# A 5th down-projection chunk as 7 block products, with the inner rows split into parts during the gate products

## The reference

```python
def swiglu_ffn(x, w_gate, w_up, w_down):
    return (jax.nn.silu(x @ w_gate) * (x @ w_up)) @ w_down      # D_FF = 2816

x = x + 0.5 * swiglu_ffn(rmsnorm(x, ffn1_norm), ...)            # ffn(0)
x = x + hybrid_mixer(rmsnorm(x, mix_norm), w_in, ...)           # attention and pooling
x = x + 0.5 * swiglu_ffn(rmsnorm(x, ffn2_norm), ...)            # ffn(1)
```

## Time and profile before

| | |
|---|---|
| Median of 3 runs | 703.39 us (703.12 to 704.21) |
| The profiled execution's own time | 703.74 us |
| Its span (first to last instruction) | 701.9 us |
| Granted TensorE clock, mean | 0.997 of full speed |
| TensorE busy | 692.2 us, 99% of the span |
| VectorE, ScalarE, GpSimd busy | 529.3, 397.4, 98.2 us |
| Read from HBM | 127.79 MB |

### The profile page before, as it was taken

How to read it: one execution, slowest core, us unless ns; L and a number is a source line. 1 busy time by engine, 2 the same in 40 slices (tenths; PEclk the granted TensorE clock), 3 DMA queues, 4 the chain that set the end, 5 groups by cost and what they waited for, 6 DMA issues and landing times.

```text
span 701.9 us, 9837 instructions
## 1 busy us (share of the span) xinstructions
PE 692.2 (99%) x3716; PEld 590.1 (84%) x3716; DVE 529.3 (75%) x774; ACT 397.4 (57%) x536; POOL 98.2 (14%) x72
## 2 busy tenths in 40 slices
PE   8999999999999999999999999999999999999995
PEld 7888888888888788888888888888888888888884
DVE  6797779989876556876679989976762747898756
ACT  6865545576377656644555566487444625576441
POOL 0022204000001300022205000000007072140002
PEclk9999999999999999999999999999999999999998
DMA  9987552348465334754552438564763273543001
GB/s 342 359 347 262 197 194 98 142 154 322 138 263 202 120 99 150 261 181 180 183 197 102 176 122 329 210 252 169 239 242 115 82 285 134 170 161 130 1 1 60
DMA packets 21109, 129.34 MB, mean 184 GB/s; under 512 B 2504, under 2 KB 3664, under 8 KB 6864
## 3 DMA queue, kind: packets, MB, share of 16 engines
q1 hardware_dynamic: 19728, 127.51, 49.7%
q10 hardware_dynamic: 1344, 1.34, 0.6%
HBM read 127.79 MB, written 1.06 MB: 184 GB/s over the span
## 4 chain that ended last, share of the span: by engine, by line
PE 97%; DVE 1%; DMA 1%; ACT 0%; SPq 0%; issue 0%; POOL 0%; POOLq 0%; DVEq 0%
PE ps L502 24%; PE ps L467 16%; PE ps L469 15%; PE ps L468 15%; PE ps L508 13%; PE ps L487 1%; PE ps L762 1%; DMA raw<-in_first 1%; PE ps L661 1%; PE ps L1114 1%; PE ps L933 1%; PE ps L521 1%; PE ps L491 1%; PE ps L817 1%; PE ps L818 1%; PE ps L819 1%
## 5 line engine op out<-in xcount | busy, mean ns | idle before, releaser
L1671 DVE TENSOR_TENSOR wlo<-raw,whi 128x2048 fp32r<-128x2048 f32 (+1 forms) x77 | 173.7, 2267 | 23.9 <-ACT whi L1191 23.7
L1191 ACT ACTIVATE whi<-raw 128x2048 fp32r<-128x2048 f32 (+1 forms) x86 | 161.3, 1879 | 40.5 <-PE ps L469 37.3
L502 PE MATMUL ps<-xt,whi 128*128 128x512 f32 x752 | 180.1, 391 | 0.0
L502 PEld LDWEIGHTS ps<-xt,whi 128*128 128x128 f32 x752 | 138.1, 188 | 26.7
L467 PE MATMUL ps<-whi,xt 128*128 128x512 f32 (+2 forms) x340 | 135.0, 397 | 0.1
L469 PE MATMUL ps<-whi,xt 128*128 128x512 f32 (+2 forms) x340 | 130.1, 383 | 0.0
L468 PE MATMUL ps<-wlo,xt 128*128 128x512 f32 (+2 forms) x340 | 129.9, 382 | 0.0
L508 PEld LDWEIGHTS ps<-xt,wlo 128*128 128x128 f32 x752 | 96.4, 191 | 3.7
L508 PE MATMUL ps<-xt,wlo 128*128 128x256 f32 x752 | 97.5, 283 | 0.0
L1594 POOL TENSOR_TENSOR wlo<-raw,whi 128x2048 fp32r<-128x2048 f32 (+1 forms) x9 | 41.0, 4558 | 290.1 <-ACT whi L1191 290.1
L1754 DVE TENSOR_TENSOR wlo<-raw,whi 128x2048 fp32r<-128x2048 f32 x32 | 75.7, 2366 | 1.2
(11 more groups left out here) (259 smaller groups left out, 776.8 us busy)
## 6 DMA issues: line engine op xcount, KB each, us to landing
raw<-in_gu SPq DMA_DIRECT2D x41, 1024.0 KB, 4.8
raw<-in_dn SPq DMA_DIRECT2D x22, 1024.0 KB, 4.7
raw<-in_win SPq DMA_DIRECT2D x8, 1024.0 KB, 4.8
raw<-in_fqk SPq DMA_DIRECT2D x8, 1024.0 KB, 4.8
raw<-in_wout SPq DMA_DIRECT2D x4, 1024.0 KB, 5.4
raw<-in_fg SPq DMA_DIRECT2D x4, 1024.0 KB, 7.3
raw<-in_fv SPq DMA_DIRECT2D x4, 1024.0 KB, 4.7
raw<-in_fo SPq DMA_DIRECT2D x4, 1024.0 KB, 4.8
```

The source lines that it names most:

```text
L502: return pe.matmul(ps[:, banks[u], :], wh[:, k * S + u * P:k * S + (u + 1) * P], x, start=k == 0, stop=k == KD - 1)
L1191: act.activation(whi[:, c % RING, w], raw[:, c % RING, w], ACT.Copy).then_inc(hi_ready, 1)
L1671: dve.tensor_tensor(wlo[:, c % RING, w], raw[:, c % RING, w], whi[:, c % RING, w].bitcast(F32), ALU.subtract).then_inc(lo_ready, 1)
```

## The change

`SEVEN` becomes (1, 3, 5, 7, 8), so g = 8 too takes two down slots; the down stage has 16 slots, with g = 8 in 12 and 13, g = 9 in 14 and g = 10 in 15. The high parts of steps 0 to 7 get eight places in the room of `par` (the mixers' parameters), the low parts overwrite the inner rows in `work`, and steps 8 to 10 use the three places of `hth`. So nothing waits for a buffer, and the parts of steps 0 to 7 are made inside the gate loop: step 2j - 1 in pass 4j, step 2j - 2 in pass 4j + 2. Since a low part overwrites rows that GpSimd reads, it waits for `s_sum` where the step is in `SEVEN`. The sums of inner rows for g = 8 are the fifth on GpSimd and stand ahead of its `weight_sums` for g = 1. `par` is loaded behind chunk 4 of the mixer's first weights, once `resid_done` says that the first FFN is over.

```diff
-SEVEN = (1, 3, 5, 7)
+SEVEN = (1, 3, 5, 7, 8)
...
+        h_hi = h_high[:, :].rearrange("p (g c) -> p g c", g=8)
+        h_lo = h_low[:, :].rearrange("p (g s) -> p g s", g=NG)
...
-            sp.dma_start(par[:, :], a["par1"]).then_inc(par_landed, 16)
...
                 chunk(C_WIN + i, a["win"][i])
+                if i == 4:
+                    sp.wait_ge(resid_done, 4)
+                    sp.dma_start(par[:, :], a["par1"]).then_inc(par_landed, 16)
...
-                    pe.wait_ge(ht_lo, ND * f + g + 1)
+                    pe.wait_ge(ht_lo, ND * f + max(g + 1, 8))
...
+                def looped_hi(j, back):
+
+                    act.wait_ge(h_done, NG * f + 4 * j - 2 * back + 2)
+                    act.activation(h_hi[:, bass.ds(2 * j - back, 1), :].rearrange("p g c -> p (g c)"),
+                                   h_sb[:, bass.ds(4 * j - 2 * back, 2), :].rearrange("p g s -> p (g s)"), ACT.Copy).then_inc(ht_hi, 1)
...
                         silu(j, i)
-                for g in range(HTS):
-                    hidden_hi(g)
+                        if i % 2 == 0:
+                            looped_hi(j, i // 2 + 1)
+                hidden_hi(8)
...
+                    if i == 0:
+                        hidden_hi(9)
...
                 input_sums_hi(0)
+                hidden_hi(10)
                 for g in range(ND - 1):
-                    if g + HTS < ND:
-                        hidden_hi(g + HTS)
...
+                def looped_lo(j, back):
+
+                    dve.wait_ge(ht_hi, ND * f + 2 * j + back - 2)
+                    if back == 1:
+                        dve.wait_ge(s_sum, 4 * NS * f + 4 * j)
...
-                for g in range(HTS):
-                    hidden_lo(g)
+                        if i % 2 == 0:
+                            looped_lo(j, i // 2 + 1)
+                hidden_lo(8)
...
+                    if i == 0:
+                        hidden_lo(9)
...
                 input_sums_lo(0)
-                weight_sums(dve, f, 1)
+                then_sums(RING - 1)
+                hidden_lo(10)
                 for g in range(ND - 2):
                     if g in SEVEN:
                         lo(C_DN[f] + place(g) + RING)
-                    if g + HTS < ND:
-                        hidden_lo(g + HTS)
+                        then_sums(place(g) + RING)
                     if g in SEVEN[:-1]:
                         input_sums_lo(SEVEN.index(g) + 1)
...
+                if SEVEN[-1] == ND - 3:
+                    products_out()
```

More of the change, by code:

```diff
@@ L168, in build @@
         hth = sb("hth", [P, HTS, BANK], F32R)
+        with nc.sbuf_tensor("more_sums", [P, HTS, BANK], F32) as more_sums:
+            pass
         htl = sb("htl", [P, HTS, BANK], F32R)
         gains = sb("gains", [P, 4, D])
+        with nc.sbuf_tensor("h_high", [P, PA_N], F32R) as h_high:
+            pass
         par = sb("par", [P, PA_N])
+        with nc.sbuf_tensor("h_low", [P, NG * S], F32R) as h_low:
+            pass
         work = sb("work", [P, 7700])
@@ L213, in build, with hidden_high @@
         s_sums = XN[:, :, :].rearrange("p t n -> p (t n)").rearrange("p (j n) -> p j n", j=4)
-        sums_hi = [xt[:, 2 * j:2 * j + 2, 0, :] for j in range(NS)]
-        sums_lo = [xt[:, 2 * j:2 * j + 2, 1, :] for j in range(NS)]
+        s_sums_of = [s_sums[:, j, :] for j in range(4)] + [more_sums[:, 2, :]]
+        sums_hi = [xt[:, 2 * j:2 * j + 2, 0, :] for j in range(4)] + [htl[:, 0, :].rearrange("p (k s) -> p k s", k=2)]
+        sums_lo = [xt[:, 2 * j:2 * j + 2, 1, :] for j in range(4)] + [htl[:, 1, :].rearrange("p (k s) -> p k s", k=2)]
+        h_hi = h_high[:, :].rearrange("p (g c) -> p g c", g=8)
+        h_lo = h_low[:, :].rearrange("p (g s) -> p g s", g=NG)
+        def hidden_high(g):
+            return h_hi[:, g, :] if g < 8 else hth[:, g - 8, :]
         part_sum = view(work, NG * S, BANK)
@@ L703, in given @@
                         col = (k * NT + t) * P
-                        return hth[:, g % HTS, col:col + P], htl[:, g % HTS, col:col + P]
+                        return hidden_high(g)[:, col:col + P], h_lo[:, 2 * g + k, t * P:(t + 1) * P]
                     def summed(i):
@@ L732, in down @@
                         m = three(ps[:, DOWN + 2 * nb + t, :],
-                                  hth[:, g % HTS, col:col + P], htl[:, g % HTS, col:col + P],
+                                  hidden_high(g)[:, col:col + P], h_lo[:, 2 * g + k, t * P:(t + 1) * P],
                                   wh[:, w], wl[:, w], g == 0 and k == 0, g == ND - 1 and k == 1)
@@ L1237, in hidden_hi @@
                 def hidden_hi(g):
-                    if g >= HTS:
-                        act.wait_ge(chunk_used, C_DN[f] + last_of(g - HTS) + 1)
                     act.wait_ge(h_done, NG * f + 2 * g + 2)
-                    act.activation(hth[:, g % HTS, :], h_sb[:, 2 * g:2 * g + 2, :].rearrange("p g s -> p (g s)"), ACT.Copy).then_inc(ht_hi, 1)
+                    act.activation(hidden_high(g), h_sb[:, 2 * g:2 * g + 2, :].rearrange("p g s -> p (g s)"), ACT.Copy).then_inc(ht_hi, 1)
+                def looped_hi(j, back):
+                    act.wait_ge(h_done, NG * f + 4 * j - 2 * back + 2)
+                    act.activation(h_hi[:, bass.ds(2 * j - back, 1), :].rearrange("p g c -> p (g c)"),
+                                   h_sb[:, bass.ds(4 * j - 2 * back, 2), :].rearrange("p g s -> p (g s)"), ACT.Copy).then_inc(ht_hi, 1)
                 if f == 0:
@@ L1282, in input_sums_hi @@
                         act.wait_ge(chunk_used, C_DN[f])
-                    act.activation(sums_hi[j], s_sums[:, j, :].rearrange("p (k s) -> p k s", k=2), ACT.Copy).then_inc(ss_hi, 1)
+                    act.activation(sums_hi[j], s_sums_of[j].rearrange("p (k s) -> p k s", k=2), ACT.Copy).then_inc(ss_hi, 1)
                 input_sums_hi(0)
+                hidden_hi(10)
                 for g in range(ND - 1):
-                    if g + HTS < ND:
-                        hidden_hi(g + HTS)
                     if g in SEVEN:
@@ L1599, in input_sums @@
                 (a11, a21), (a12, a22) = ([h_sb[:, 2 * g + k, t * P:(t + 1) * P] for t in range(NT)] for k in range(2))
-                s1, s2, s3, s4 = (s_sums[:, j, i * P:(i + 1) * P] for i in range(4))
+                s1, s2, s3, s4 = (s_sums_of[j][:, i * P:(i + 1) * P] for i in range(4))
                 before = 4 * (NS * f + j)
@@ L1726, in hidden_lo @@
                     dve.wait_ge(ht_hi, ND * f + g + 1)
-                    dve.tensor_tensor(htl[:, g % HTS, :], h_sb[:, 2 * g:2 * g + 2, :].rearrange("p g s -> p (g s)"), hth[:, g % HTS, :].bitcast(F32),
-                                      ALU.subtract).then_inc(ht_lo, 1)
+                    if g in SEVEN:
+                        dve.wait_ge(s_sum, 4 * (NS * f + SEVEN.index(g) + 1))
+                    dve.tensor_tensor(h_lo[:, 2 * g:2 * g + 2, :].rearrange("p g s -> p (g s)"), h_sb[:, 2 * g:2 * g + 2, :].rearrange("p g s -> p (g s)"),
+                                      hidden_high(g).bitcast(F32), ALU.subtract).then_inc(ht_lo, 1)
+                def looped_lo(j, back):
+                    dve.wait_ge(ht_hi, ND * f + 2 * j + back - 2)
+                    if back == 1:
+                        dve.wait_ge(s_sum, 4 * NS * f + 4 * j)
+                    pair = bass.ds(4 * j - 2 * back, 2)
+                    dve.tensor_tensor(h_lo[:, pair, :].rearrange("p g s -> p (g s)"), h_sb[:, pair, :].rearrange("p g s -> p (g s)"),
+                                      h_hi[:, bass.ds(2 * j - back, 1), :].rearrange("p g c -> p (g c)").bitcast(F32), ALU.subtract).then_inc(ht_lo, 1)
                 sum_halves(0, 0)
@@ L1765, in input_sums_lo @@
                     dve.wait_ge(ss_hi, NS * f + j + 1)
-                    dve.tensor_tensor(sums_lo[j], s_sums[:, j, :].rearrange("p (k s) -> p k s", k=2), sums_hi[j].bitcast(F32), ALU.subtract).then_inc(ss_lo, 1)
+                    dve.tensor_tensor(sums_lo[j], s_sums_of[j].rearrange("p (k s) -> p k s", k=2), sums_hi[j].bitcast(F32), ALU.subtract).then_inc(ss_lo, 1)
                 def half(t, nb, p, scale=0.5):
@@ L1795, in products_out, with then_sums @@
                     ordered(dve.scalar_tensor_tensor(out=second, in0=part_sum.unsqueeze(1).broadcast_to([P, 2, BANK]), scalar=0.5, in1=second, op0=ALU.mult, op1=ALU.add))
+                def then_sums(slot):
+                    for j in range(1, NS):
+                        if place(SEVEN[j]) == slot + 1:
+                            weight_sums(dve, f, j)
                 input_sums_lo(0)
-                weight_sums(dve, f, 1)
+                then_sums(RING - 1)
+                hidden_lo(10)
                 for g in range(ND - 2):
@@ L1808, in ffn @@
                         lo(C_DN[f] + last_of(g) + RING)
-                    if g in SEVEN[:-2]:
-                        weight_sums(dve, f, SEVEN.index(g) + 2)
+                        then_sums(last_of(g) + RING)
+                if SEVEN[-1] == ND - 3:
```

(1 more changed line is left out.)

## The result

The changed kernel takes 707.12 us (median of 5 runs, 706.90 to 707.51); before took 704.16 over its 5 runs, the 3 shown above and 2 made beside the changed kernel. The ratio is 1.0045, 95% interval 1.0030 to 1.0059: slower by 0.45%, where 706.5 us and 0.44% were forecast. In a later set the changed kernel stood at 1.0052 (1.0039 to 1.0066). The spans of the profiled executions, 705.5 and 701.9, differ by 3.6 us, where the sum gave 3.1. The granted clock is 0.998, before it was 0.997.

What follows compares the result with a forecast made beforehand. TensorE, busy 99% of the span, was taken to bound the kernel. Per FFN -0.74 + 1.0 + 1.3 = +1.56 us, +3.1 in all, giving 706.5 us against 703.39, slower by 0.44%, range 704.3 to 709.2.

Steps and rivals of the forecast that it cites:

- The gain: TensorE's down stage: three matmuls fewer, -0.68 us, and the 0.06 wait in seven(7) gone; -0.74 us per FFN.
- The first gap: seven(1): TensorE waits for the sums' low part, as GpSimd's later weight sums delay DVE in pass 19; 1.0 us per FFN.
- The second gap: seven(8): TensorE waits for the sums' low part, queued behind lo of slot 14 on DVE; 1.3 us per FFN.
- the gate loop: Parts made inside the gate loop: DVE and ACT have room for them in the passes; 0 us.
- the load of `par`: Mixers' parameters, 2 MB, loaded late: lands early enough to be hidden, with the DMA engines nearly idle; 0 us.
- The rest of the down stage: Down stage outside the two gaps: DVE's load hardly grows and products_out comes no later against TensorE; 0 us.
- Only the second gap: Rival: DVE has caught up by seven(1), so only seven(8) waits; +0.56 us per FFN, 704.5 us; chance 0.13.
- no gap: Rival: sums' low parts come in time in seven(1) and seven(8), only matmuls count; 701.9 us, faster; chance 0.09.
- `par` in the way: Rival: the parameters' load delays the mixer's chunks 5 to 7, TensorE short 2 to 4 us; 708.5 to 710.5; chance 0.06.
- Whole blocking: Rival: DVE loses all 5.38 us of GpSimd's additions, gap in seven(1) 2.3; +2.9 per FFN, 709.2 us; chance 0.10.

Runs made afterwards that it cites:

- e3_both: Changed kernel with both reorderings: sums' parts for g = 8 ahead of slot 14, GpSimd's weight sums ahead of its fifth input sums; 701.97 us, 0.9979 of before.
- e8_dve_sums_second: Changed kernel with sums' parts for g = 8 ahead of slot 14, and weight sums of g = 1 on DVE instead of GpSimd; 701.88 us, 0.9979 of before.
- e9_both_again: e3_both repeated on another chip: the changed kernel with both reorderings; 701.93 us, 0.9975 of before.
- e4_four: Changed kernel without its fifth step: g = 8 an ordinary step again, the rest of the change kept; 703.34 us, 0.9997 of before.
- e2_first: Changed kernel with only GpSimd's order changed: weight sums for g = 1 ahead of the fifth input sums; 704.87 us, 1.0018 of before.
- e7_dve_sums: Changed kernel with the weight sums of g = 1 moved from GpSimd to DVE, behind pass 19; 704.75 us, 1.0023 of before.
- e5_late_parts: Changed kernel with DVE's two added low parts, hidden_lo(8) and hidden_lo(9), moved behind input_sums_lo(0); 706.19 us, 1.0039 of before.
- e1_second: Changed kernel with only the order at g = 7 changed: sums' high and low parts for g = 8 ahead of slot 14's; 704.61 us, 1.0009 of before.
- e6_more_load: Changed kernel with three more 0.5 MB loads behind that of par, whose readers wait for them too; 707.24 us, 1.0055 of before.

## Why the prediction was right

**The gain.** -0.74 per FFN was forecast. No run shows it alone, but e3_both, e8_dve_sums_second and e9_both_again, which have no gap, lie 1.5 to 1.6 us below before, against twice 0.74. The 0.06 in it is gone as well (e4_four).

**The first gap.** Taken at 1.0, measured 1.26. The mechanism was as written: pass 19, beside L370, and e2_first and e7_dve_sums close it by moving or removing GpSimd's additions. The term that was mis-sized is DVE's loss in pass 19: 4.02 was carried over from pass 17, it was 8.25 - 3.86 = 4.39. `times_row` alone makes the difference, 2.86 instead of 2.50: it began 0.46 us behind GpSimd's first addition then (108.09 to 108.55) and only 0.09 behind it now (119.42 to 119.51), so it met more of it. GpSimd was that late because its fifth input sums had met DVE's low part of pass 18: L1625 took 0.91, where the same line takes 0.46 in pass 16, and DVE's L1759 took 0.95 instead of 0.69. The sum allowed 0.1 to 0.3 for that meeting as time of DVE; this time itself did no harm, as DVE stood 0.60 ahead of pass 19, and the delay of GpSimd did. The low part of the sums ended at 136.97, for 136.75 in the text, and TensorE's second matmul followed 0.40 later, for 0.39. The rest of the difference is TensorE itself, which in this trace was 0.16 us earlier than in that of before. What the section does not say is that the two low parts, 1.2 us in its sum, are as much a condition of the gap as GpSimd's place: without them it is 0.06 (e5_late_parts).

**The second gap.** Worked out as 1.3, measured 1.35, and e1_second closes it by the order of the queue alone. The step said that it doesn't hang on how late DVE is otherwise, save for a bound of 1.5 with DVE 0.2 late. That was too strong: in e5_late_parts DVE came later and the gap was 1.89.

**Costs put at nothing.** All held: the gate loop and the load of `par` (e4_four, e6_more_load). `par` landed in 7.2 to 7.7 us. For the gate loop, DVE did stand 2.14 us for GpSimd's sums at the end of pass 16, where 1.6 was taken, and no one waited for it. The rest of the down stage was put at nothing as well and held in the changed kernel, but e5_late_parts shows how near to its end that room is.

**The rivals.** Only the second gap, and no gap, are refuted by the trace, and both exist as kernels: e2_first (1.0018) and e3_both (0.9979). `par` in the way is refuted by e6_more_load. Whole blocking was to show as 5.38 lost and a first gap of 2.3; it was 4.39 and 1.26. That refutes the price and not the rule: the additions' recorded durations sum to 5.39, but L372 began 0.47 us before `times_row` had ended and L374 0.20 before `hidden` had, so GpSimd's durations seem to hold waits of its own and can't be added up as DVE's loss. By the Trainium skill (SBUF — State Buffer, Who interferes with whom) the loser blocks for the whole instruction. The trace agrees: `times_row` began 0.09 behind L370 and ended 0.55 behind its end, `lo` began 0.13 behind L374 and ended 2.15 behind its end. Each is 0.14 short of what the instruction takes alone (0.69 and 2.29).

**The size.** The sum gave 3.1, the balance of the trace is 3.7, the spans 3.6, the medians 3.0 to 3.8. That the first ratio, 1.0045, meets the forecast of 0.44% to a hundredth is luck: the two gaps were taken 0.31 us per FFN too small, before stood at 704.16 in this comparison and not at the 703.39 that the forecast started from, and the changed kernel stood at 1.0052 in the next set. The 0.2% by which the kernel could have been faster was lost to two new waits, each as long as almost two such gains.

## What to carry to other kernels

When a step is made cheaper on the bounding engine, look in each helper's queue at what stands ahead of the one instruction that the shortened step waits for; moving it ahead of one copy and one subtraction was worth 2.8 us here, twice the gain of the whole change. Putting two shortened steps next to each other takes away the long step that had stood between them; that this long step had hidden the helper's chain is read from the order of the queue, and no run here has the fifth step in another place. And work given to GpSimd isn't free for DVE: count what DVE loses beside it before counting what it saves.

## What the runs showed of the hardware that was not expected

Three additions (one of 1024 and two of 512 elements per partition, float32, from and to SBUF) take DVE 2.58 us. On GpSimd they took 5.4, beside a busy DVE, and cost DVE 4.4 us of its own time: DVE's instructions with both inputs in SBUF stretched beside them (0.69 to 2.86, 0.42 to 1.51, 2.29 to 3.38), while L1733, which has one input in PSUM, kept its 0.69. I had not expected that leaving them to the helper was dearer, for the engine that was to be relieved, than doing them.
